# Attention with a side job: four whole modulation items, or eight items by kind, in other units

## What is computed

```
h = rmsnorm(x, norm1) * (1 + scale1) + shift1
proj = h @ w_in                      # queries (low rank), keys and values (low rank), rope key, pooling input
attn = softmax(q k^T * scale) v      # 8 heads; latent queries read 1024 latent and 128 cached keys,
                                     # context queries read the 128 context keys
x = x + gate1 * (concat(attn, pooled) @ w_o)
h2 = rmsnorm(x, norm2) * (1 + scale2) + shift2
x = x + gate2 * (square(relu(h2 @ w1)) @ w2)
y = rmsnorm(x, final_norm)
```

## Time and profile before

| | us |
|---|---|
| runs of the kernel before | 1417.91, 1419.39, 1422.32; median 1419.39 |
| the profiled execution's own time | 1418.45 |
| its span | 1416.7 |
| TensorE busy (matmuls) | 1366.8 (96%) |
| VectorE busy | 789.7 (56%) |
| ACT busy | 700.9 (49%) |
| GpSimd busy | 432.6 (31%) |

### The profile page before, as it was taken

One profiled execution on the slowest core, in us unless ns is written; L12 is line 12 of the kernel. 1 busy time (PEld: TensorE's weight loads), 2 busy tenths in 40 slices (PEclk: granted clock), 3 DMA queues, 4 the chain that ended last, 5 costly groups with the idle time before them and its releaser, 6 DMA issues.

```text
span 1416.7 us, 20384 instructions
## 1 busy us (share of the span) xinstructions
PE 1366.8 (96%) x7548; PEld 1227.8 (87%) x7548; DVE 789.7 (56%) x1066; ACT 700.9 (49%) x1409; POOL 432.6 (31%) x533
## 2 busy tenths in 40 slices
PE   7999989999899899999999999999999999999996
PEld 2899879999888888899998889999999999999995
DVE  4777677777667654255554456543445565344444
ACT  4867577787777633243333443433334443333332
POOL 3366648787878444440000002200000030000002
PEclk9999999999999999999999999999999999999999
DMA  9431101111111250254443333433333334333321
GB/s 345 147 99 53 35 25 43 43 43 33 30 38 38 75 200 1 81 216 148 155 173 132 119 120 119 176 135 118 118 137 125 124 120 163 128 138 119 118 89 45
DMA packets 50492, 154.63 MB, mean 109 GB/s; under 512 B 9848, under 2 KB 12440, under 8 KB 50424
## 3 DMA queue, kind: packets, MB, share of 16 engines
q1 hardware_dynamic: 49560, 150.60, 30.1%
q0 software_dynamic: 864, 3.15, 0.5%
HBM read 148.73 MB, written 4.83 MB: 108 GB/s over the span
## 4 chain that ended last, share of the span: by engine, by line
PE 63%; POOL 1%; DMA 0%; DVE 0%; issue 0%; ACT 0%; SPq 0%; DVEq 0%; POOLq 0%
PE bank L2068 28%; PE bank L2076 28%; PE bank L1789 7%; PE bank L1551 1%; DMA x<-in_w_o 0%; POOL x L1859 0%; PE bank L2090 0%; POOL stat L1863 0%; POOL stat L1883 0%; DVE wol L1746 0%; ACT woh L1715 0%; SPq L1671 0%; DVE x L2019 0%; DVE xn L2007 0%; POOL stat L1865 0%
## 5 line engine op out<-in xcount | busy, mean ns | idle before, releaser
L2068 PE MATMUL bank<-h2h,w1l 128*128 128x384 f32 x768 | 258.2, 336 | 0.0
L2068 PE MATMUL bank<-h2l,w1h 128*128 128x384 f32 x768 | 258.2, 336 | 0.0
L2068 PE MATMUL bank<-h2h,w1h 128*128 128x384 f32 x768 | 258.1, 336 | 0.0
L1859 POOL TENSOR_TENSOR x<-x,xn 128x512 f32<-128x512 f32 x12 | 20.6, 1746 | 726.5 <-DVE rTl L1977 499.8
L1966 DVE TENSOR_TENSOR w2l<-w2raw,w2h 128x1024 fp32r<-128x1024 f32 x95 | 118.7, 1249 | 169.5 <-ACT w2h L1897 169.5
L1897 ACT ACTIVATE w2h<-w2raw 128x1024 fp32r<-128x1024 f32 x95 | 100.8, 1061 | 191.3 <-PE bank L2076 191.3
L1904 ACT ACTIVATE relu<-bank 128x384 f32<-128x384 f32 x94 | 46.2, 491 | 287.6 <-PE bank L2068 287.6
L2076 PE MATMUL bank<-w2h,rTh 128*128 128x512 f32 x576 | 181.8, 396 | 0.0
L2076 PE MATMUL bank<-w2l,rTh 128*128 128x512 f32 x576 | 179.3, 392 | 0.0
L2076 PE MATMUL bank<-w2h,rTl 128*128 128x512 f32 x576 | 178.2, 390 | 0.0
L1973 DVE TENSOR_TENSOR sq<-relu 128x384 f32<-128x384 f32 x96 | 57.1, 595 | 179.5 <-ACT relu L1904 174.7
(11 more groups left out here) (272 smaller groups left out, 2748.4 us busy)
## 6 DMA issues: line engine op xcount, KB each, us to landing
w1raw<-in_w SPq DMA_DIRECT2D x96, 512.0 KB, 3.8
w2raw<-in_w SPq DMA_DIRECT2D x96, 512.0 KB, 4.6
ada_raw<-in_w_ada SPq DMA_DIRECT2D x24, 512.0 KB, 5.3
xn<-in_w_ada SPq DMA_DIRECT2D x16, 512.0 KB, 3.8
xin<-in_x SPq DMA_DIRECT2D x9, 512.0 KB, 3.8
x<-in_x SPq DMA_DIRECT2D x3, 1536.0 KB, 9.4
g_raw<-in_w_ada SPq DMA_DIRECT2D x8, 512.0 KB, 3.8
x<-in_w_o SPq DMA_DIRECT2D x6, 512.0 KB, 6.0
```

Source lines behind the costliest of these rows:

```text
L1859: nc.gpsimd.tensor_tensor(k.x[:, t, cut], k.x[:, t, cut], gated_half(t, i), ALU.add).then_inc(out_added, 1)
L2068: op = nc.tensor.matmul(bank[6 + s][:, 0:BN], w[0][s][x][:, c * P:(c + 1) * P], k.h2[b % 2][y_][:, c, :], start=n == 0, stop=n == 3 * DC - 1)
```

## The change

Each item becomes two, the context's kind first (`acc[1]`), then the latent kind (`acc[0]`), of four matmuls each. They stand in units 18, 21, 34, 37, 50, 53, 63 and 64; the blocks stand in units 4, 7, 10, 13, 20, 23, 26, 29, 36, 39, 42, 45, 52, 55, 58, 61. The context's item waits only for the context's additions of the group's last block, and GpSimd starts a new group's context sum after the context's item and its latent sum after the latent item. The two additions on VectorE per item become one for each of twice as many. The order of the ring follows from `MOD_AT`.

```diff
--- before.py
+++ after.py
@@ -322,8 +322,8 @@
         SIDE_AT = {0: ("k", 0), 1: ("q", 0), 3: ("k", 1), 4: ("q", 1), 5: ("k", 2), 7: ("q", 2)}
         NADA = 16
         ADA0 = 3 * DC
-        ADA_AT = {4 + 15 * r // 4: r for r in range(NADA)}
-        MOD_AT = {15 * g + 18: g for g in range(NADA // 4)}
+        ADA_AT = {at: r for r, at in enumerate((4, 7, 10, 13, 20, 23, 26, 29, 36, 39, 42, 45, 52, 55, 58, 61))}
+        MOD_AT = {u: n for n, u in enumerate((18, 21, 34, 37, 50, 53, 63, 64))}
         CTX_AT = {3: "scores", 5: "turn", 7: "values"}
         KEY_BANK, QUERY_BANK, VALUE_BANK = (bank[0], bank[1], bank[3]), (bank[6], bank[4], bank[5]), (bank[6], bank[5], bank[7])
         KEY_ITEM, QUERY_ITEM = (2, 3, 4), (1, 5, 6)
@@ -393,7 +393,7 @@
                 pe.wait_ge(side_freed, side_read(kind, j))
                 return
             freed, value = {"turn": (t_lo, j + 1), "q": (q_nope, j + 1), "ctx_scores": (c_exp, j + 1), "ctx_turn": (c_low, 2 * j + 1),
-                            "ctx_values": (c_low, 2 * j + 2), "mod": (mod_read, 2 * j + 2)}[kind]
+                            "ctx_values": (c_low, 2 * j + 2), "mod": (mod_read, j + 1)}[kind]
             pe.wait_ge(freed, value)
 
         def ctx_now(u, what):
@@ -497,7 +497,7 @@
                         sp.dma_start(k.xn[:, 0, :], a["w_ada"][ADA0 + r]).then_inc(ada_loaded, 16)
                     if u % 4 == 0 and u:
                         spread(u // 4 - 1)
-                sp.wait_ge(mod_read, 2 * (NADA // 4))
+                sp.wait_ge(mod_read, len(MOD_AT))
                 for n in range(2):
                     sp.dma_start(k.xn[:, n, :], a["w_o"][W_O[n]]).then_inc(k.wo_loaded[n], 16)
 
@@ -616,12 +616,14 @@
                         at = DC + 2 * (r % 4) + c
                         nc.gpsimd.tensor_scalar(prod[:, c, :], ada_raw[:, c, :], k.sf[:, at:at + 1], None, ALU.mult).then_inc(ada_prod, 1)
                     if r % 4 == 0 and r:
-                        pool.wait_ge(mod_filled, r // 4)
+                        pool.wait_ge(mod_filled, r // 2 - 1)
                     pool.wait_ge(ada_prod, 2 * r + 2)
                     ada_add(r, acc[1], prod, 4 * r)
 
                 def ada_latent(r):
                     pool.wait_ge(ada_lat, 2 * r + 2)
+                    if r % 4 == 0 and r:
+                        pool.wait_ge(mod_filled, r // 2)
                     ada_add(r, acc[0], ada_raw, 4 * r + 2)
 
                 def ada_add(r, to, terms, done):
@@ -1119,13 +1121,12 @@
                     dve.wait_ge(c_filled, 3 * h + 1)
                     nc.vector.tensor_reduce(cnm[:, :], ring_bank("ctx_scores", h)[:, 0:P], AX_X, ALU.max, negate=True).then_inc(c_nm, 1)
 
-                def modulation(g):
-                    at = ADA0 + 4 * g
-                    b = ring_bank("mod", g)[:, 0:8].rearrange("p (c j) -> p c j", j=2)
-                    dve.wait_ge(mod_filled, g + 1)
-                    for j in range(2):
-                        nc.vector.tensor_tensor(k.mod[:, at:at + 4, j], b[:, :, j], k.cols[:, C_BADA + at:C_BADA + at + 4],
-                                                ALU.add).then_inc(mod_read, 1)
+                def modulation(n):
+                    at, j = ADA0 + 4 * (n // 2), 1 - n % 2
+                    b = ring_bank("mod", n)[:, 0:8].rearrange("p (c j) -> p c j", j=2)
+                    dve.wait_ge(mod_filled, n + 1)
+                    nc.vector.tensor_tensor(k.mod[:, at:at + 4, j], b[:, :, j], k.cols[:, C_BADA + at:C_BADA + at + 4],
+                                            ALU.add).then_inc(mod_read, 1)
 
                 def rope_rows(j, lo, hi, highs):
                     dve.wait_ge(setup_hi, highs)
@@ -1420,14 +1421,13 @@
                                                   start=n == 0 and m == 0 and r == 0, stop=n == KI - 1 and r == 1)
                     op.then_inc(pv_done, 1)
 
-                def modulation(g):
-                    b = ring_bank("mod", g)
-                    pe.wait_ge(ada_sums, 16 * g + 16)
-                    ring_free(pe, "mod", g)
+                def modulation(n):
+                    b, j = ring_bank("mod", n), 1 - n % 2
+                    pe.wait_ge(ada_sums, 16 * (n // 2) + 14 + 2 * (n % 2))
+                    ring_free(pe, "mod", n)
                     for c in range(4):
-                        for j in range(2):
-                            op = nc.tensor.matmul(b[:, 2 * c:2 * c + 2], acc[j][:, c * P:(c + 1) * P], k.sel[:, j, :],
-                                                  start=j == 0, stop=j == 1)
+                        op = nc.tensor.matmul(b[:, 2 * c:2 * c + 2], acc[j][:, c * P:(c + 1) * P], k.sel[:, j, :],
+                                              start=True, stop=True)
                     op.then_inc(mod_filled, 1)
 
                 def scores_ctx(h):
```

## The result

The changed kernel took 1425.97 us (median of 7 runs, 1425.74 to 1430.69) where the kernel before, run beside it, took 1420.44 (7 runs, 1417.91 to 1424.12): a ratio of 1.0044, 95% interval 1.0029 to 1.0059. It is 5.5 us slower, more than the 0.3% that can be told from no change (the interval's lower end lies at that bound), and half a microsecond above 1425.5, the top of the predicted range. The prediction had given a slower kernel a chance of 0.14. Its profiled execution took 1430.69 us, the slowest of the seven, with a span of 1428.9.

The account below looks back on a forecast made before the run. TensorE's own work bounds the kernel. Units 11 to 55: 2.15 + 5.3 + 3.1 = 10.5 for 11.5 now, -1.0; end +1.65; +0.7 us in all, median 1420.1, own range 1416.5 to 1423.5, outer 1413.5 to 1425.5.

Parts of the forecast that it names:

- Where the waits stand: Turns wait some 1.2 us for VectorE's key in units 22, 38, 54; ACT idles for GpSimd in 15, 31, 47.
- The ring's term: Units 22, 38 and 54: a turn of TensorE waits for VectorE's key four places before, each unit 1.4 us longer.
- The item at place 5: Half item in units 21, 37, 53, after the context's turn: about 0.67 us hides in slack, 0.27 is left each.
- The late blocks: GpSimd's blocks three units apart slip: unit 15 pays 2.15 us, units 31 and 47 0.55 + 1.0 each, 3.1 together.
- The rule: A late block's scaling on ACT lengthens its unit by 0.55 us plus ACT's wait, 1.3 in unit 15.
- the chain of loads: Unit 13's block: GpSimd's steps before it end near 240.2, its load lands at 244.0, its products are ready at 247.1.
- the groups of units 20 and 36 slip less: Units 31 and 47: additions in one instruction and longer units 22, 38, so ACT waits 1.0 us, not 1.3.
- The end of the stage: Last block moved to unit 61: last inverse and the exchange of sums 1.65 us later, bounds 0 and 3.5.
- (B): Rival, chance 0.16: products ready over 2 us into a unit, ACT waits 2.5 in units 15, 31, 47, 63; 1425.4.
- (A): Rival, chance 0.17: the ring's wait is hidden, GpSimd keeps pace, only 0.55 us per block stays; -8 us, 1411.
- (C): Rival, chance 0.12: the skewed order changes nothing, the exponential's chain takes back whatever TensorE wins; 1419.4 us.
- that pairing: VectorE's L1263 while GpSimd runs L617, before units 24, 40, 56: costs nothing; by the skill's rule about 2 us more.

Follow-up runs that it names:

- e3: The kernel before with one unused ring place behind the context's turn in units 21, 37 and 53, no work added: 1423.14 us, ratio 1.0018.
- e2: The changed kernel with the third and fourth block of the first three groups one and two units later, items unchanged: 1419.77 us, ratio 0.9989.
- e7: e2 with the last group of blocks in units 51, 54, 57, 60 and the sixth item in unit 52: 1417.07 us, ratio 0.9978.
- e8: The changed kernel without any edit, measured and profiled a second time (the column "again"): 1426.47 us, ratio 1.0044.
- e6: The changed kernel with ACT's scaling and GpSimd's last additions one unit later for the blocks of units 13, 29 and 45: 1419.09 us, ratio 0.9998.
- e5: The kernel before with the change's block places and whole items in units 18, 34, 50 and 64: 1428.17 us, ratio 1.0059.
- e1: The changed kernel with the items of units 21, 37 and 53 moved to units 20, 36 and 52: 1426.76 us, ratio 1.0044.
- e4: The kernel before with e7's block places and whole items in units 18, 34, 50 and 63: 1416.14 us, ratio 0.9969.

## Why the prediction was wrong

The forecast was +0.7 us, measured were +5.5. The mechanism was right; terms of the sum were too small, by 1.5 us the item's at place 5 and by 1.1 the late blocks', by about 0.3 the end's, and the fall of the clock had no term. Set against the second profile, in which no fall follows a wait, step by step:

- **Where the waits stand** was right. Turns waiting for the key in units 22, 38, 54; ACT waiting for GpSimd in 15, 31, 47; units 33, 43, 48, 49 at their ordinary length. The ring's term was 1.4 a head and is 1.4 to 1.5, shown alone in e3.
- **The item at place 5** was mis-sized: 0.27 forecast, 0.76 measured, 1.5 us in three heads. I let a half item hide in the slack as a whole one had at place 2. It doesn't: the item has a wait of its own, 0.23 us, for the turn four places before it, and then its matmuls take 1.02. I had asked what is late behind the item and not what the item waits for.
- **The late blocks**. Forecast 2.15, 1.55 and 1.55 above 4.96; measured in "again" 2.4 (with 0.06 in unit 14), 2.3 and 1.7, 1.1 us more in all. The rule, ACT's stall plus 0.55, held: the stalls are 1.72, 1.62 and 1.02, so it gives 2.27, 2.17 and 1.57. For unit 15 the chain of loads was right too: products were forecast at 247.1, and measured, less the 3.57 us by which unit 2 started later, at 247.4, so that ACT stood for 1.7 and not 1.3. The 0.3 for a late query in unit 14 came to 0.06, though ACT did wait for it. The step that failed is that the groups of units 20 and 36 slip less: in unit 31 ACT stands for 1.6 us, not 1.0.
- **The end of the stage**: 1.65 forecast, 1.9 and 3.3 measured in the two profiles. e2 against e7 gives 1.6 for the last block's unit. In the first profile more comes on top: ACT stands 0.66 us for GpSimd in unit 63 (0.43 in e8), where I had none. What else separates 3.3 from 1.9 stays open.
- **The clock** had no term at all, neither in the sum nor in a rival, and it adds 1.5 us for each fall in the first profile. I had priced only ACT's stall, and not noted that it makes TensorE stand still for 2 us ahead of its values.
- Without falls these terms give 13.6 us come (2.4 + 2.3 + 1.7 for blocks, 3 x (0.13 + 0.76 + 1.5) for items and ring) in place of 10.5, for 11.5 gone: +2.1, and units 2 to 62 measured +2.4. With 1.9 at the end this is +4.3. Between the medians are 5.5 and 6.1. What is left, 1.2 to 1.8, fits how often the clock falls, behind waits or in units 0 and 1. No trace shows these in the other runs, but each run has its mean granted clock on record. Among the runs with 0.991 to 0.994 the kernel before has a median of 1421.5 (36 of the 58 runs beside the experiments) and the changed kernel 1426.0 (13 of 17): 4.5 us apart, near the sum's 4.3. Of the rest, 20 of the 58 have 0.995 or more, at 1417.9, and only 1 of the 17; and 3 of the 17 have 0.990, at 1430.1 or more. So part of the 5.5 lies in how often each kernel runs at the lower clock. Why the changed kernel should do so more often, when the slow stretch common to both its profiles is that of units 0 and 1, which the change doesn't touch, is open.

Of the rivals, (B) gave 1425.4, close to the measured time, and its condition was met in unit 15: the products were ready 2.1 us after that unit began. Its price wasn't: ACT stood for 1.7, 1.6, 1.1 and 0.7 us, not 2.5 each, and no late query held the units behind. It had 0.16 and deserved more, as its condition stood within 0.1 us of my own numbers: by them the products of unit 13's block were ready 247.1 - 245.14 = 1.96 us after unit 15 began. (A) is refuted by the waits, (C) by the ratio. The product L1263 of the earlier trace rows (L1264 here) took 1.07 us at 377.34 in the changed kernel too, where L617 ran from 374.89 to 378.01, and unit 40 and its like kept their length: that pairing cost TensorE nothing, as the rows had it. It isn't free for GpSimd in the other order (last section).

## What to carry to other kernels

Price an item that moves in a rotating ring from both sides: what it waits for (the item one turn of the ring before it) and what will now wait for it, and find for each the instruction that frees it. When a producer is late, look at what stands behind the wait on the engine that is waiting: here 1.7 us of ACT became 2.4 us of TensorE, while the same lateness cost 0.6 with the waiting step one unit later (e6). And where the granted clock can fall, a wait that leaves the busiest engine idle is worth more than its length: give it a term, or at least a place in the range.

## What the runs showed that I had not expected

- The clock falls behind some waits of TensorE and not behind others of the same length: after 2.07 and 1.99 us in one execution, and not after 2.12 and 2.02 in the other, same kernel. e5 has a stretch of ten microseconds at 0.50.
- Units 0 and 1 took 14.5 to 14.6 us in five profiles (before, e1, e4, e5, e6) and 17.6 in five (after, e2, e3, e7, e8), though their code is the same in all. In the five slow ones unit 0 began at 166.2 us or later, in the others at 165.7 or earlier. Why is open; it moves the time of a run by 3 us and blurs every comparison of this kernel by some of that. The five profiles with slow units have mean granted clocks of 0.990 to 0.993, four of the others 0.996 or 0.997 (the fifth is e5, with its long fall at the end), so the mean clock of a run hints at which kind it was.
- Where an instruction of VectorE and one of GpSimd with two SBUF inputs each overlap in the rows below, the one that starts second is the longer for it. In the changed kernel VectorE's product L1264 begins behind GpSimd's L582 and takes 1.42 us instead of 1.07; GpSimd's last additions, 2.65 us for two beside most work, begin behind that product and take 3.35:

```profile
256.20 0.87 POOL L582 TENSOR_TENSOR whl<-whr,whh 128x320 fp32r<-128x320 f32 x1
256.51 1.42 DVE L1264 TENSOR_TENSOR attn<-ropeq,out_l 64x512 f32<-64x512 f32 x1
257.03 3.35 POOL L636 TENSOR_TENSOR xn<-xn 128x512 f32<-128x512 f32 x2
```

At 493.87 the product meets the first of two additions only at its very end and begins ahead of the second: VectorE takes 1.08 us, and the two additions 3.47. With L617, which has one tensor as input, only one order matters: the product isn't longer behind it (1.07 us at 377.34), but the second instruction of L617 at 216.74, begun 0.79 us into the product of 215.95, took 1.68 us instead of 1.57.

The Trainium skill ("SBUF — State Buffer", section "Who interferes with whom") has a VectorE instruction with two SBUF inputs contend with a GpSimd instruction that reads SBUF. For the additions and L582, which have two SBUF inputs, the trace agrees, with 0.7 us for GpSimd and 0.35 for VectorE; for L617 it agrees where L617 starts second, with 0.1 us, and not where the product does.
